# Token tiles in eight slots with two-engine evictions, and the third modulation row inside the first projection wave, in a one-core diffusion-block kernel

## What is computed

```python
h_c = rms_norm(ctx, norm_mix_g[l])
sh_c, sc_c = adaln(c_ctx, w_mod[l], b_mod[l], 2)
p_c = (h_c * (1.0 + sc_c) + sh_c) @ w_in[l][:, K_COL:]
...
sh, sc, g, sh2, sc2, g2 = (m[:, None, :] for m in adaln(c, w_mod[l], b_mod[l], 6))
h = rms_norm(x, norm_mix_g[l]) * (1.0 + sc) + sh
y, _, _ = hybrid_mixer(h @ w_in[l], lat_chunks, ...)
x = x + g * y
h2 = rms_norm(x, norm_ffn_g[l]) * (1.0 + sc2) + sh2
x = x + g2 * expert_choice_ffn(h2, w_router[l], w_gate_e[l], w_up_e[l], w_down_e[l], cap_lat)
return rms_norm(x, final_g)
```

## Time and profile before

| What | Value |
|---|---|
| median of 3 runs | 1822.85 us (1822.5 to 1828.38) |
| profiled execution | 1822.42 us, its span 1820.6 us |
| TensorE | 1693.1 us busy, 93% of the span |
| VectorE, ScalarE, GpSimd | 1332.4, 1041.1 and 145.5 us busy |
| DMA | 492.80 MB, mean 271 GB/s |
| the chain that ended last | TensorE 89%, VectorE 6%, ScalarE 2% |
| mean granted clock of TensorE | 0.973 |

### The profile page before, as it was taken

How to read it: one execution, slowest core, us unless ns; L and a number is a source line. 1 busy time by engine, 2 the same in 40 slices (tenths; PEclk the granted TensorE clock), 3 DMA queues, 4 the chain that set the end, 5 groups by cost and what they waited for, 6 DMA issues and landing times.

```text
span 1820.6 us, 21564 instructions
## 1 busy us (share of the span) xinstructions
PE 1693.1 (93%) x8088; PEld 1347.7 (74%) x8096; DVE 1332.4 (73%) x1295; ACT 1041.1 (57%) x955; POOL 145.5 (8%) x137
## 2 busy tenths in 40 slices
PE   5989999999699817999999999999999999999995
PEld 2578997878544415888888888888888888888884
DVE  2556544317732377898898898898898898898887
ACT  5253212245611124777777777777777777777775
POOL 3001100002000001011011011011011011011010
PEclk9999999999899967999999999999999999999998
DMA  9115531120042247999999999999999999999996
GB/s 340 49 32 182 166 105 48 47 88 6 3 155 88 99 179 262 365 388 369 385 388 367 383 389 368 384 390 367 390 384 367 391 382 368 390 380 369 391 381 242
DMA packets 204423, 492.80 MB, mean 271 GB/s; under 512 B 5700, under 2 KB 18792, under 8 KB 204376
## 3 DMA queue, kind: packets, MB, share of 16 engines
q1 hardware_dynamic: 188128, 436.35, 64.3%
q0 software_dynamic: 13248, 47.09, 8.6%
q10 hardware_dynamic: 3000, 8.70, 1.2%
HBM read 471.07 MB, written 21.05 MB: 270 GB/s over the span
## 4 chain that ended last, share of the span: by engine, by line
PE 89%; DVE 6%; ACT 2%; issue 1%; DMA 1%; ACTq 0%; DVEq 0%; POOL 0%; POOLq 0%
PE ps L1008 85%; PE ps L1377 2%; PE ps L1340 1%; DVE topi L1817 1%; DVE topv L1816 1%; DVE affT L1819 1%; DVE ring L1900 0%; PE ps L1026 0%; DVE hs L1719 0%; ACT h2T L906 0%; DVE wl L1867 0%; PE ps L1296 0%; DMA xe<-ffn_in,idx_e 0%; ACT raw L705 0%; DMA vecs<-in_mlstm_norm_g 0%
## 5 line engine op out<-in xcount | busy, mean ns | idle before, releaser
L1867 DVE TENSOR_TENSOR wl<-ring,wh 128x2048 fp32r<-128x2048 f32 x384 | 877.7, 2290 | 110.9 <-ACT wh L952 110.7
L952 ACT ACTIVATE wh<-ring 128x2048 fp32r<-128x2048 f32 x384 | 736.9, 1920 | 286.4 <-PE ps L1008 286.4
L1008 PE MATMUL ps<-wh,xel 128*128 128x512 f32 x1024 | 408.0, 398 | 1.4 <-DVE xel L1847 1.4
L1008 PE MATMUL ps<-wh,xeh 128*128 128x512 f32 x1024 | 401.6, 392 | 0.0
L1008 PE MATMUL ps<-wl,xeh 128*128 128x512 f32 x1024 | 400.9, 391 | 0.0
L1008 PEld LDWEIGHTS ps<-wh,xeh 128*128 128x128 f32 x1024 | 192.4, 188 | 44.9
L1008 PEld LDWEIGHTS ps<-wh,xel 128*128 128x128 f32 x1024 | 192.6, 188 | 42.7 <-DVE xel L1847 1.8
L1008 PEld LDWEIGHTS ps<-wl,xeh 128*128 128x128 f32 x1024 | 192.7, 188 | 41.1
L1008 PE MATMUL ps<-wh,hidl 128*128 128x512 f32 x512 | 204.0, 398 | 0.0
L1008 PE MATMUL ps<-wh,hidh 128*128 128x512 f32 x512 | 200.8, 392 | 0.0
L1008 PE MATMUL ps<-wl,hidh 128*128 128x512 f32 x512 | 200.3, 391 | 0.0
(11 more groups left out here) (353 smaller groups left out, 1955.4 us busy)
## 6 DMA issues: line engine op xcount, KB each, us to landing
ring<-in_w_gate_e SPq DMA_DIRECT2D x64, 2048.0 KB, 8.8
ring<-in_w_up_e SPq DMA_DIRECT2D x64, 2048.0 KB, 8.5
ring<-in_w_down_e SPq DMA_DIRECT2D x64, 2048.0 KB, 10.2
mbw<-in_w_mod POOLq DMA_DIRECT2D x32, 512.0 KB, 5.2
hpr<-in_w_in SPq DMA_DIRECT2D x12, 1024.0 KB, 5.2
moda<-in_w_mod SPq DMA_DIRECT2D x4, 2048.0 KB, 19.6
xs<-in_x POOLq DMA_DIRECT2D x8, 512.0 KB, 6.7
ring<-in_w_out SPq DMA_DIRECT2D x2, 2048.0 KB, 7.9
```

Of the source, the lines that this page charges most:

```text
L952: act.activation(whv[m % 4], eview(m), ACT.Copy).then_inc(hi_done, 1)
L1008: return pe.matmul(o, l, r, start=start, stop=stop)
L1867: dve.tensor_tensor(wlv[m % 4], eview(m), whv[m % 4].bitcast(F32), ALU.subtract).then_inc(lo_done, 1)
```

## The change

Slots: `xs` becomes eight tiles. Slots 4 to 7 lie where the second buffer of projection weights (`hpr1`, `hph1`) lies later. GpSimd issues tiles 0 and 1, then its constants, then tiles 2 to 7, then the gathers for the gates, then tiles 8 and 9 as slots come free. SyncE starts modulation piece 0 at once, pieces 2 and 3 once tile 7 has landed, and the second weight piece once eight tiles are transposed. GpSimd's loads of the second modulation part also wait for modulation piece 3.

Evictions: `norm_copy` on ScalarE evicts the first bank of a tile, the new `token_copy` on VectorE the second, each with its own semaphore; TensorE waits for both.

Order: row 0 stands behind tile 2 on TensorE, row 1 behind tile 5 and the columns of row 0, the columns of row 1 before tile 9. Row 2 leaves the head's list and stands behind step 0 of the wave; the columns of row 2 and the products of row 3 move behind step 1. The transposes of `wsraw` move behind step 5. On ScalarE the first square stands before the Silu of the conditioning vectors, the copy of `wgr` moves from tile 6 to tile 7, `piece_high(0)` from tile 8 to behind the root of tile 9, and `hch` comes before `wsT`. On VectorE the subtraction for `wgl` moves behind the eviction half of tile 7, and `mod_copy(2)`, `mod_bias(2)` and `mod_copy(3)` move back.

```diff
--- before.py
+++ after.py
@@ -75,6 +75,7 @@
     def pbank(g):
         return g if g < WAVE else (g - WAVE) % 4
 
+    XS = 8
     MSLOT = 2
     ESLOT = 4
     GUC = DE // W
@@ -154,7 +155,7 @@
         wgl = at(VTR, "wgl", [P, KT, P], F32R)
         wgh = at(VTR + 4 * KB, "wgh", [P, KT, P], F32R)
         mrow = at(VTR + 8 * KB, "mrow", [2, MOD_A, W])
-        xs = at(YMR, "xs", [P, 4, D])
+        xs = [at(o + i % 4 * 4 * KB, f"xs{i}", [P, D]) for i, o in enumerate([YMR] * 4 + [RA + 16 * KB] * 4)]
 
 
         ygT = at(YG, "ygT", [P, H, T])
@@ -283,7 +284,7 @@
         ws_in = sem("ws_in")
         bs_in = sem("bs_in")
         gates_in = sem("gates_in")
-        x_in = [sem(f"x_in{i}") for i in range(4)]
+        x_in = [sem(f"x_in{i}") for i in range(XS)]
         mod_in = [sem(f"mod_in{i}") for i in range(MOD_A)]
         hp_in = [sem(f"hp_in{i}") for i in range(2)]
         hp_hi = sem("hp_hi")
@@ -302,7 +303,8 @@
         ss_ready = sem("ss_ready")
         xn_ready = sem("xn_ready")
         xt_ready = sem("xt_ready")
-        xt_free = sem("xt_free")
+        xt_free_a = sem("xt_free_a")
+        xt_free_v = sem("xt_free_v")
         vec_t = sem("vec_t")
         vcol_ready = sem("vcol_ready")
         scol_ready = sem("scol_ready")
@@ -437,8 +439,8 @@
         NVEC = row
 
 
-        HEAD_PE = "t0 t1 t2 t3 r0 t4 t5 c0 r1 t6 t7 t8 t9 c1 r2".split()
-        HEAD_DVE = "t0 t1 t2 t3 t4 t5 r0 t6 t7 c0 t8 r1 t9 c1".split()
+        HEAD_PE = "t0 t1 t2 r0 t3 t4 t5 c0 r1 t6 t7 t8 c1 t9".split()
+        HEAD_DVE = "t0 t1 e0 t2 e1 t3 e2 r0 t4 e3 t5 e4 c0 t6 e5 t7 r1 e6 t8 e7 g t9 e8 c1 e9".split()
         STEPS = [(j, d) for j in range(NT) for d in range(2)]
         NS = len(STEPS)
         NSU = NS - 2
@@ -463,38 +465,43 @@
 
             return ps[:, 4 + b, 0:2 * V1].rearrange("p (a v) -> p a v", v=V1)
 
-        XS_TURNS = [len(range(i, NTC + NT, 4)) for i in range(4)]
+        XS_TURNS = [len(range(i, NTC + NT, XS)) for i in range(XS)]
 
         block = es.enter_context(nc.Block())
 
         @block.gpsimd
         def _(pool):
             link = chain(pool, pool_step)
-            for t in range(4):
+
+            def head_consts():
+                link(pool.memset(ident[:], 0.0))
+                link(pool.affine_select(out=ident[:], in_=ident[:], compare_op=ALU.not_equal, fill=1.0, base=0,
+                                        pattern=[[-1, P]], channel_multiplier=1))
+                pool.memset(ones[:], 1.0)
+                pool.memset(epsc[:], EPS)
+                pool.tensor_copy(identb[:], ident[:])
+                pool.memset(floorc[:], LOG_INV_SCALE)
+                pool.memset(raw[:, 0:1], 0.0)
+                pool.memset(raw[:, T + 1:T + 2], 0.0)
+                pool.memset(rawc[:, 0:1], 0.0)
+                pool.memset(rawc[:, TC + 1:TC + 2], 0.0)
+                link(pool.memset(gbias[:], 0.0))
+                link(pool.memset(wgr[:], 0.0))
+                pool.sem_inc(consts_in, 1)
+
+            for t in range(XS):
                 src = cf[t * P:(t + 1) * P, :] if t < NTC else xf[(t - NTC) * P:(t - NTC + 1) * P, :]
-                pool.dma_start(xs[:, t, :], src).then_inc(x_in[t], 16)
-            link(pool.memset(ident[:], 0.0))
-            link(pool.affine_select(out=ident[:], in_=ident[:], compare_op=ALU.not_equal, fill=1.0, base=0,
-                                    pattern=[[-1, P]], channel_multiplier=1))
-            pool.memset(ones[:], 1.0)
-            pool.memset(epsc[:], EPS)
-            pool.tensor_copy(identb[:], ident[:])
-            pool.memset(floorc[:], LOG_INV_SCALE)
-            pool.memset(raw[:, 0:1], 0.0)
-            pool.memset(raw[:, T + 1:T + 2], 0.0)
-            pool.memset(rawc[:, 0:1], 0.0)
-            pool.memset(rawc[:, TC + 1:TC + 2], 0.0)
-            link(pool.memset(gbias[:], 0.0))
-            link(pool.memset(wgr[:], 0.0))
-            pool.sem_inc(consts_in, 1)
+                pool.dma_start(xs[t][:], src).then_inc(x_in[t], 16)
+                if t == 1:
+                    head_consts()
             for n in range(4):
                 src = w_in[0][:, G0 + H * n:G0 + H * (n + 1)].rearrange("(k p) n -> p k n", p=P)
                 pool.dma_start(wgr[:, :, 32 * n:32 * n + H], src).then_inc(gates_in, 16)
                 b = (b_igate, b_fgate)[n // 2][0, n % 2].rearrange("(h a) -> h a", a=1)
                 pool.dma_start(gbias[32 * n:32 * n + H, :], b).then_inc(gates_in, 16)
-            for t in range(4, NTC + NT):
-                pool.wait_ge(xt_ready, t - 3)
-                pool.dma_start(xs[:, t % 4, :], xf[(t - NTC) * P:(t - NTC + 1) * P, :]).then_inc(x_in[t % 4], 16)
+            for t in range(XS, NTC + NT):
+                pool.wait_ge(xt_ready, t - XS + 1)
+                pool.dma_start(xs[t % XS][:], xf[(t - NTC) * P:(t - NTC + 1) * P, :]).then_inc(x_in[t % XS], 16)
             link(pool.memset(maskb[:], 0.0))
             link(pool.memset(onesel[:], 0.0))
             pool.affine_select(out=onesel[:], in_=onesel[:], compare_op=ALU.not_equal, fill=1.0, base=0,
@@ -508,6 +515,7 @@
 
 
             pool.wait_ge(xt_ready, NTC + NT)
+            pool.wait_ge(mod_in[MOD_A - 1], 16)
 
             def mod_load(q):
                 i, k = q // MBQ, 2 * (q % MBQ)
@@ -610,13 +618,14 @@
                 a = MOD_ORDER[n] * W
                 sp.dma_start(moda[n][:], wmod[:, :, a:a + W]).then_inc(mod_in[n], 16)
 
-            sp.wait_ge(x_in[1], 16)
             mod_piece(0)
             sp.wait_ge(x_in[3], 16)
             mod_piece(1)
             half_piece(0)
+            sp.wait_ge(x_in[7], 16)
             mod_piece(2)
             mod_piece(3)
+            sp.wait_ge(xt_ready, XS)
             half_piece(1)
 
             sp.wait_ge(pj_free, NH2)
@@ -680,18 +689,26 @@
                 n = v.shape[0] // P
                 act.dma_start(vecs[VROW[name]:VROW[name] + n, :], v.rearrange("(r p) -> r p", p=P)).then_inc(vecs_in, 16)
             act.dma_start(wsraw[:], gmlp_ws[0].rearrange("h p q -> p h q")).then_inc(ws_in, 16)
+            def square(t):
+                act.wait_ge(x_in[t % XS], 16 * (t // XS + 1))
+                if t >= 1:
+                    act.wait_ge(ss_ready, t)
+                return act.activation(raw[:, 1:1 + D], xs[t % XS][:], ACT.Square, accum_out=stat[:, 0, t:t + 1])
+
+            act.wait_ge(consts_in, 1)
+            link(square(0))
             act.wait_ge(vcol_ready, 1)
             act.activation(scol[:].rearrange("p k c -> p c k"),
                            vcol[:, VROW["c"]:VROW["c"] + 2 * KT].rearrange("p (c k) -> p c k", c=2),
                            ACT.Silu).then_inc(scol_ready, 1)
-            act.wait_ge(consts_in, 1)
 
             def norm_copy(t):
 
                 act.wait_ge(xt_ready, t + 1)
                 dst = hcr[:, :, t * P:(t + 1) * P] if t < NTC else hTr[:, :, (t - NTC) * P:(t - NTC + 1) * P]
                 b = 2 * (t % 2)
-                act.activation(dst, two(b, b + 2).rearrange("p (k t) -> p k t", k=KT), ACT.Copy).then_inc(xt_free, 1)
+                act.activation(dst[:, 0:KT // 2], ps[:, b, :].rearrange("p (k t) -> p k t", k=KT // 2),
+                               ACT.Copy).then_inc(xt_free_a, 1)
 
             def piece_high(i):
 
@@ -699,27 +716,25 @@
                 act.activation(hph[i % 2][:], hpr[i % 2][:], ACT.Copy).then_inc(hp_hi, 1)
 
             for t in range(NTC + NT):
-                act.wait_ge(x_in[t % 4], 16 * (t // 4 + 1))
                 if t >= 1:
-                    act.wait_ge(ss_ready, t)
-                link(act.activation(raw[:, 1:1 + D], xs[:, t % 4, :], ACT.Square, accum_out=stat[:, 0, t:t + 1]))
+                    link(square(t))
                 act.activation(stat[:, 1, t:t + 1], stat[:, 0, t:t + 1], ACT.Sqrt, bias=epsc[:],
                                scale=1.0 / D).then_inc(ss_ready, 1)
                 if t >= 1:
                     norm_copy(t - 1)
-                if t == 6:
+                if t == 7:
                     act.wait_ge(gates_in, 8 * 16)
                     act.activation(wgh[:], wgr[:], ACT.Copy).then_inc(hp_hi, 1)
-                if t == 8:
+                if t == 9:
                     piece_high(0)
             norm_copy(NTC + NT - 1)
             for k in range(KT):
                 act.wait_ge(h_mod, k + 1 if k < KT // 2 else k + 1 + KT // 2)
                 act.activation(hTh[:, k], hTr[:, k], ACT.Copy).then_inc(h_hi, 1)
+            act.wait_ge(h_mod, 2 * KT)
+            act.activation(hch[:], hcr[:], ACT.Copy).then_inc(h_hi, 1)
             act.wait_ge(ws_t, 1)
             act.activation(wsT[:], ps[:, 6, :].rearrange("p (h q) -> p h q", h=H), ACT.Copy).then_inc(wsT_ready, 1)
-            act.wait_ge(h_mod, 2 * KT)
-            act.activation(hch[:], hcr[:], ACT.Copy).then_inc(h_hi, 1)
 
             def take(g, dst, src, f=ACT.Copy):
                 act.wait_ge(pj_done, g + 1)
@@ -1021,10 +1036,11 @@
 
                 pe.wait_ge(xn_ready, t + 1)
                 if t >= 2:
```

(50 more changed lines are left out.)

## The result

The changed kernel took 1830.49 us (median of 11 runs, 1826.13 to 1832.52); the kernel before, in the same sessions, 1825.96 (11 runs, 1822.5 to 1828.81). The ratio is 1.0022, with a 95% interval of 1.0014 to 1.003: **slower by 4.0 us, between 2.6 and 5.5**. It was forecast unchanged, at 1822.4, in a range up to 1828. Part of the miss in microseconds is the reference: the three runs shown first had a median of 1822.85, eleven have one 3.1 us higher. The other part, the 4.0 us, is the change.

What follows compares the result with a forecast made beforehand. The chain of waits bounds the kernel; only the head can move, and busy TensorE behind it passes changes through one for one. Terms 0.7 − 3.8 + 4.4 − 1.3 = 0.0 on 1822.42 gave 1822.4 us, range 1817.5 to 1828.

Steps and rivals of the forecast that it cites:

- Term 1: Head up to the end of row 1: row 0 earlier, row 1 starting as before, possibly a colder clock; +0.7 us.
- term 2: From row 1's end to the wave's start: 15.7 us in place of 19.5, so −3.8 us.
- term 3: Wave's start to the mark (first context group's start): row 2 and a cold start come in, the hcl wait goes; +4.4 us.
- term 4: Behind the mark (first context group's start): the cold start of TensorE's clock there goes; −1.3 us.
- Rival (d): Head's start: vectors land 2 us late and one more table load (1.28 us) comes in; 1825.7 us, chance 0.13.
- the hole and its cold start: TensorE's 4.8 us wait for hcl before the first context group, and the low clock after it (1.3 us), both go.
- the idle 6 us ahead of the wave: Before the wave, TensorE idles about 6 us while VectorE prepares step 0, as no row keeps it busy.
- the price of the third row: Row 2 inside the wave: 6.96 us of products without cover, plus 2.2 us for a cold start.
- the exchange as a whole: Head: a 4.8 us hole and its cold start traded for an uncovered row and another cold start; sum 0.0.
- The transfers: Modulation piece 1 lands at 31 us, before row 1 needs it at 31.5; hidden, with half a us of cover.
- (b): Rival, faster: no chain behind row 0, row 1 starts when modulation piece 1 is in; 1816.1 us, chance 0.10.
- (c): Rival, slower: gathers of wgr slow the transfers, piece 1 lands at 39, row 1 6.8 us late; 1829.2 us, chance 0.09.

Runs made afterwards that it cites:

- Experiment 3: The changed kernel with modulation piece 0 issued only after tile 1 has landed: 1832.9 us, ratio 1.0043 to the kernel before.
- Experiment 4: The changed kernel with the Silu ahead of the first square again: 1827.89 us, ratio 1.001 to the kernel before.
- experiment 2: The changed kernel with row 2 back ahead of the wave, 0.9983; also the kernel before, hch copied ahead of wsT, with row 2 inside the wave, 1.0001.
- experiments 4, 5 and 6: The changed kernel, singly: Silu ahead of the first square, 1.001; GpSimd's masks written later, 1.0023; row 0 behind tile 3 again, 1.0014.
- experiment 1: The kernel before with only hch copied ahead of wsT and the wsraw transposes moved behind the wave's step 5: 1818.79 us, ratio 0.9968.

## Why the prediction was wrong

**Term 1 failed, the end of row 1: forecast +0.7, measured +6.6, and the step in it that failed is its start.** The rest held: term 2 came out at −3.8 (15.7 us from row 1's end to the wave, as forecast), term 3 at +3.8 (forecast +4.4), term 4 at −1.3 or so (the clock at the mark is 1.00). The sum of the head is +5.4 where I had 0.0; the runs gave +4.0, between 2.6 and 5.5. Of the 5.9 us that term 1 was off:

- *The start*, 3.6 us (row 0 at 22.6, forecast 19.0). I took the vectors' landing as what opens the work and the first square, moved ahead of it, as a gain of 1.05 us. In fact tile 0 landed at 8.8 and opened it. The first table load, hidden at 3.99 us before, stood behind that landing, and a third one came in. The first root came 2.4 us later than before, where the forecast had it 1.05 earlier: 3.45 us. Experiment 3 shows the part of the early piece 0: with tile 0 landed at 5.4 the same three loads gave a root at 11.3, 0.7 earlier than before. Experiment 4 shows the part of the order: 1.3 us. The error was to count the square as moved from behind to ahead of a wait without asking what its own wait, and the table load in front of it, would become, and to take it that tiles and piece 0 share the queues from their issue on as they do at 20 us.
- The masks added 1.0 us on VectorE, a term that I didn't have: I had followed GpSimd's list up to the gathers, but not what moves up behind them when the waits for slots go. The quick transposes of tile 2 (1.09 us; 1.97 in experiment 2 with the same code) made up for 0.9 of it in this execution.
- *Behind row 0*, 6.5 us to row 1 where I had 5.5, and *row 1*, 9.07 us for 6.96. Both are the clock of this one execution: tile 5's transposes took 1.97 us and the columns 0.51, and the granted clock there was 0.50. With the same code up to tile 9, experiment 2 has 5.5 and 6.96 us, as forecast, behind a row 0 of 7.43 that began at 23.5. There the start is the whole of the miss, and row 1 ended 4.2 us behind the forecast.

Rival (d), with a chance of 0.13 and 1825.7 us, was the nearest. Its third load came. Its other half, vectors 2 us late, did not: they were 0.9 us late and not what ended last. That its 3.3 us are close to the 3.45 is luck in part.

What I had right: the hole and its cold start (5.8 us in the runs), the idle 6 us ahead of the wave, and the price of the third row. I had 6.96 + 2.2 against a wave that starts 2.5 us earlier, 6.7 in all; experiment 2 has 8.7 against 1.85, 6.9. It is the exchange as a whole that brings nothing, since the hole can be closed without it. The transfers were right for piece 1 (no wait for it in the trace). Rivals (b) and (c) didn't happen; a late modulation piece, which (c) feared for piece 1 by the gathers, appeared for piece 0 in experiment 3, by the tiles.

Open: how the 3 to 4 us of the tile part divide. The ratios of experiments 4, 5 and 6 (2.2, −0.2 and 1.5 us) are each within reach of nothing, and single profiles differ by up to 1.8 us with the same code. What decides which row starts cold is not known. A kernel with eight slots and piece 0 issued between tiles 0 and 1 was not tried.

## What to carry to other kernels

A block of work without dependencies is worth most where its engine would idle: moved from an idle stretch into a full one, it costs about its whole length (6.9 and 7.7 us here for a row of 6.96). Before a first instruction is moved ahead of a wait, look at what its own wait is, and at the table load in front of it. And when waits are taken out of a queue, everything behind them runs earlier, and may meet another engine at its ports. Two profiles of the same code are the measure of what a difference between two profiles is worth.

## What was not expected of the hardware

- With a 2 MB transfer of the SyncE queue issued 0.5 us ahead, the first tile of GpSimd's queue moved no byte until 5 us, 3.7 us after its issue (before: 0.63 MB between 2 and 5 us); its landing went from 4.3 to 7.5 us. Later, with both in full flow, q0 moved 68 packets and 0.22 MB between 7 and 8 us, q1 73 and 0.15.
- The same VectorE instruction (128x1024 scaling) took 0.75 us in most places, and 1.82 and 0.98 beside GpSimd's writes of the masks (0.80 and 0.75 once these were moved). It took 1.18 once in experiment 4, while GpSimd issued its last gathers; no run tests that one.
- The same code gave a cold row or not. With the head of before, row 0 took 6.96 us in the kernel before and 7.78 in experiment 1; with the changed head, rows 0 and 1 took 6.96 and 9.07 in one execution and 7.43 and 6.96 in another. In experiments 4 and 5 they took 9.02 and 6.96, and 7.91 and 7.55.
- Row 0 has only transposes and gaps ahead of it. In the kernel before and in the changed one its products started 0.43 us apart from the first on, the spacing at the upper level. So transposes did bring the clock there, against the rule that the prediction weighed, but not every time: the first gaps were 0.85 us in experiments 1, 4 and 5.
